# Down-projection of a dense SwiGLU layer: activation splits placed ahead of weight splits, and one chunk instead of two half-size chunks at the head of each half

## The chip, the cores and the metric

The kernel runs as one program on one core of a Trainium2 chip. The metric is the device time of one execution in microseconds (us), from launch to the last output. The core has a matrix engine (TensorE, PE in the profile; its weight loads are PEld), three elementwise engines (VectorE is DVE, ScalarE is ACT, GpSimd is POOL) and SyncE (SP), which here issues the transfers from device memory. Each engine takes its own instructions strictly in the order of the program and waits on counting semaphores that other engines raise.

## The reference, cut to what matters

Two layers of a diffusion backbone over 256 latent and 256 context tokens, all in float32. Layer 0 ends in a dense SwiGLU, layer 1 in a mixture of experts. The change touches only the last matrix product of the dense SwiGLU, that of `wd`:

```python
D_MODEL = 1024; SEQ = 256; CTX_LEN = 256; D_FF = 2816

def swiglu(h, wg, wu, wd):
    return (jax.nn.silu(h @ wg) * (h @ wu)) @ wd

# layer 0, for the latent tokens x and the context tokens ctx alike:
f_x = swiglu(ln_modulate(x, sh2x, sc2x), w_ff_gate[0], w_ff_up[0], w_ff_down[0])
x = ln_affine(ALPHA * x + gt2x * f_x, ln2_g[0], ln2_b[0])
```

## The kernel before, in words

A float32 product is made of three faster ones: each operand is split into a high part (a rounded copy) and a low part (operand minus high part), and `mm3` (L836) issues high x high, high x low and low x high. So every weight chunk must be split before TensorE can use it. ScalarE copies it to `w_hi` (`split_hi`, L1594), and then VectorE makes three quarters of `w_lo` and GpSimd the last quarter, at the same time (the two `split_lo`, L2020 and L2620). `w_lo` lies over `ring`, where the chunk landed. The ring has 4 slots of 2048 floats per partition (1 MB), `w_hi` has 3 buffers (HIS). The activations `a_t` of the down-projection are split too: `down_hi` on ScalarE (L1850) and `down_lo` on VectorE (L2312) write `a_hi` and `a_lo`, two buffers each.

The inner dimension 2816 is 22 tiles of 128 (FT). `DOWN` cuts it into six groups: one of 2 tiles at the head, then five of 4. The product is made in two halves, first the latent tokens (half 1), then the context tokens (half 0), with all weights read twice. So there are 12 groups, g = 0 to 11, and g = 6 is the head of the second half. A group has two chunks, dh = 0 and 1, one for each half of the 1024 output columns. A chunk of a full group is 4 tiles x 512 columns (1 MB) and takes 4 tiles x 2 token blocks x 3 = 24 matmuls; a chunk of a head group is 2 tiles x 512 columns (512 KB) and takes 12. q_down is the number, among all split chunks, of the first chunk of the down-projection.

What sets the order, engine by engine:
- TensorE waits at each group for `as_hi` and `as_lo` (the activations are split) and at each chunk for `lo_dve` and `lo_pool` (the weights are split). The last matmul of a chunk raises `w_used`; at the end of a half that matmul raises `fd_mm` instead, and `w_used` comes with the next matmul.
- ScalarE and VectorE run, for each group g: the splits of the two chunks of group g + 1, then the split of the activations of group g + 1, and in the second half a piece of the residual addition and layer norm of the latent tokens (`add_half`, `norm_a`, `norm_b`, `modulate`).
- `split_hi(q)` waits until chunk q - 3 is used, since it takes that chunk's `w_hi` buffer. The split of the second chunk of group g + 1 therefore waits for the first chunk of group g. `down_hi(g)` waits until group g - 2 is used.
- SyncE loads chunk n into the ring when chunk n - 4 is used. GpSimd runs its parts of the splits one after another.
- Ahead of the down-projection, the first two of its chunks are split inside the loop over gate and up projections. The second of these on VectorE stands between the last activation product (L2305) and `down_lo(0)`.
- In group 10 TensorE transposes the two normed latent tiles (`turn_tile`, the second one behind the second chunk); the second waits for `modulate` of the first tile on ScalarE and VectorE (`h_t`, L1624 and L2039). After the down-projection it goes on to the input projection of layer 1 for the latent tokens, with weights `in_w_in`.

Of the kernel before, what the change touches and what calls it, by code (L numbers as in the profile page):

```python
# [30 lines left out]
D = 1024  # L31
# [20 lines left out]
FT = D_FF // P  # L52
# [182 lines left out]
def ring_chunks(w):  # L235

    chunks = []

    def mod(l, cb):
        v = w["w_mod"][l].rearrange("(h k p) n -> h p k n", h=2, p=P)  # L240
        for h in range(2):
            chunks.append((("mod", l, cb, h), [(0, (4, 512), v[h, :, :, cb * 512:(cb + 1) * 512])]))

    def rows(name, v, k, c0, n):
        chunks.append((name, [(0, (k, n), v.rearrange("(k p) n -> p k n", p=P)[:, :, c0:c0 + n])]))

    for cb in EARLY_MOD:
        mod(0, cb)
    for l in range(DEPTH):
        w_in = w["w_in"][l]  # L250
        in_cols = ((0, Q_LORA), (OFF_KV, KV_LORA + ROPE), (OFF_F, 2 * FC), (OFF_F + 2 * FC, 2 * FC))
        for ch in IN_ORDER[l]:
            rows(("in", l, ch), w_in, KD, *in_cols[ch])
        if l == 0:
            for cb in FOURIER_MOD.values():
                mod(0, cb)
        for g in range(4):
            uq = w["w_uq"][l].rearrange("(k p) n -> p k n", p=P)[:, :, g * 4 * QK:(g + 1) * 4 * QK]
            uk = w["w_uk"][l][:, g * 4 * NOPE:(g + 1) * 4 * NOPE]
            uv = w["w_uv"][l][:, g * 4 * VH:(g + 1) * 4 * VH]  # L260
            chunks.append((("heads", l, g), [(0, (2, 4 * QK), uq), (2 * 4 * QK, (256,), uk),
                                             (2 * 4 * QK + 256, (256,), uv)]))
        for u, (kind, jj) in enumerate(MERGE):
            src, k, c0 = {"ga": (w_in, KD, OFF_G), "gf": (w_in, KD, OFF_G + D), "ao": (w["w_ao"][l], KD, 0),
                          "fo": (w["w_fo"][l], FG, 0)}[kind]
            rows((kind, l, jj), src, k, c0 + jj * 256, 256)
            if u in MERGE_MOD:
                mod(l, MERGE_MOD[u])
        v = w["w_out"][l].rearrange("(g k p) n -> g p k n", k=4, p=P)
        for dh in range(2):  # L270
            for kk in range(2):
                chunks.append((("out", l, dh, kk), [(0, (4, 512), v[kk, :, :, dh * 512:(dh + 1) * 512])]))
        if l == 0:
            for fp in range(FT // 2):
                rows(("fg", fp), w["w_ff_gate"][0], KD, fp * 256, 256)
                rows(("fu", fp), w["w_ff_up"][0], KD, fp * 256, 256)
                if 2 <= fp < 8:
                    mod(1, fp - 2)
            down = w["w_ff_down"][0].rearrange("(f p) n -> p f n", p=P)
            for half in (1, 0):  # L280
                for fg, n in DOWN:
                    for dh in range(2):
                        chunks.append((("fd", half, fg, dh), [(0, (n, 512), down[:, fg:fg + n, dh * 512:(dh + 1) * 512])]))
    return chunks

DOWN = [(0, FT % 4)] + [(f, 4) for f in range(FT % 4, FT, 4)]
assert FT % 4 and FT % 2 == 0  # L290


IN_ORDER = ((0, 1, 2, 3), (0, 2, 3, 1))
# [46 lines left out]
def build(nc, w, out):  # L340
    ctx = ExitStack()
    with ctx:
# [95 lines left out]
        a_hi = over("a_hi", [P, 2, 4, SEQ], at_a)  # L438
# [158 lines left out]
        w_used = sem("w_used")  # L597
# [224 lines left out]
        def _(pe):  # L822
# [373 lines left out]
            def dense_mixer():  # L1196
# [17 lines left out]
                for hx, half in enumerate((1, 0)):  # L1214
                    for i, (fg, n) in enumerate(DOWN):
                        g = len(DOWN) * hx + i
                        if g == 0:
                            pe.wait_ge(mod_done, mod_at[(1, 5)] + 1)
                        pe.wait_ge(as_hi, g + 1)
                        pe.wait_ge(as_lo, g + 1)  # L1220
                        for dh in range(2):
                            v = split_chunk(("fd", half, fg, dh), (n, 512))
                            order = [(f, t) for f in range(n) for t in range(2)]
                            if i == len(DOWN) - 1:
                                order = [(f, t) for t in range(2) for f in range(n)]
                            for f, t in order:
                                end = fg + f == FT - 1
                                cols = slice(t * P, (t + 1) * P)
                                mm3(psum[:, ff_bank(2 * half + t, dh), :],
                                    (a_hi[:, g % 2, f, cols], a_lo[:, g % 2, f, cols]), [x[:, f, :] for x in v],  # L1230
                                    start=(fg + f == 0), stop=end, sig=fd_mm if end else None,
                                    free=w_used if (f, t) == order[-1] else None)
                            if half == 0 and i == 4:
                                turn_tile(2, dh, 2 + dh)

# [335 lines left out]
        def _(act):  # L1571
# [129 lines left out]
            for l in range(DEPTH):  # L1701
# [133 lines left out]
                if l == 0:  # L1835
# [14 lines left out]
                    def down_hi(g):  # L1850

                        fg, n = DOWN[g % len(DOWN)]
                        c0 = SEQ if g < len(DOWN) else 0
                        if g >= 2:
                            act.wait_ge(w_used, q_down + 2 * (g - 1))
                        act.wait_ge(fa_done, fg + n)
                        act.activation(a_hi[:, g % 2, 0:n, :], a_t[:, fg:fg + n, c0:c0 + SEQ], ACT.Copy).then_inc(as_hi, 1)

                    act.wait_ge(fu_mm, FT)
                    down_hi(0)  # L1860
                    for g in range(2 * len(DOWN)):
                        for q in (q_down + 2 * g, q_down + 2 * g + 1):
                            if q + 2 < q_end:
                                split_hi(q + 2)
                        if g + 1 < 2 * len(DOWN):
                            down_hi(g + 1)
                        i = g - len(DOWN)
                        n = stats_before[2]
                        if i in (1, 2):
                            std(n + i - 1)  # L1870
                        elif i == 3:
                            std(n + 2)
                            std(n + 3)
                        elif i in (4, 5):
                            modulate(1, 1, i - 2, tiles_before[2] + i - 4)
# [103 lines left out]
        def _(dve):  # L1979
# [163 lines left out]
            for l in range(DEPTH):  # L2143
# [151 lines left out]
                if l == 0:  # L2295
# [21 lines left out]
                        low(a_lo[:, g % 2, 0:n, :], a_t[:, fg:fg + n, c0:c0 + SEQ], a_hi[:, g % 2, 0:n, :]).then_inc(as_lo, 1)  # L2317

                    down_lo(0)
                    for g in range(2 * len(DOWN)):  # L2320
                        for q in (q_down + 2 * g, q_down + 2 * g + 1):
                            if q + 2 < q_end:
                                split_lo(q + 2)
                        if g + 1 < 2 * len(DOWN):
                            down_lo(g + 1)
                        i = g - len(DOWN)
                        n = stats_before[2]
                        if i == 0:
# [447 lines left out]
```

## Time and profile before

| | |
|---|---|
| time, median of 3 runs | 2342.35 us (2335.09 to 2345.68) |
| the profiled execution: its time | 2342.66 us |
| its span, first to last instruction | 2340.8 us |
| mean granted TensorE clock | 0.946 |
| TensorE busy / VectorE busy / ScalarE busy / GpSimd busy | 90% / 41% / 32% / 26% |
| the down-projection | 840.06 to 986.10 us, 528 matmuls of 128x128 by 128x512 |

The profiled execution lies 0.3 us above the median of the runs, and its span is 1.9 us shorter than its time. Granted clock 1.00 means 2.4 GHz, and 0.5 means 1.2 GHz. Busy times of a matmul overlap the next one's: the distance from start to start is the true pace, 0.227 us for the 512 columns of this product at full clock.

### The profile page before, as it was taken

How to read it: one execution, taken by the hardware profiler on the slowest of the kernel's cores; microseconds unless marked ns; L12 is line 12 of the kernel's file. 1: busy time of each engine (PE TensorE's matmuls, PEld its weight loads, DVE VectorE, ACT ScalarE, POOL GpSimd, SP SyncE). 2: the span in 40 equal slices, each digit the busy share in tenths (PEclk: the TensorE clock that was granted, in tenths of full speed). 3: DMA queues.
4: the chain of work that ended last, by engine and by line, in shares of the span. 5: the costliest groups of instructions: out<-in, count | busy, mean ns of one | idle time of the engine just before them, and what ended most of it. 6: DMA issues, size and time to landing. Idle time of an engine off the chain costs nothing.

```text
span 2340.8 us, 33031 instructions
## 1 busy us (share of the span) xinstructions
PE 2095.2 (90%) x13045; PEld 1432.0 (61%) x13045; DVE 969.1 (41%) x1448; ACT 744.1 (32%) x1005; POOL 599.5 (26%) x344
## 2 busy tenths in 40 slices
PE   6988889993999988988788679999989999998886
PEld 3444467782877766755486555666565666666664
DVE  2244521256222334844423654333443323445445
ACT  2035532233121233324533222233232223333442
POOL 0012312150122234202323213333212333233431
PEclk8999999995999999999899779999999999999997
DMA  7311025440254334411067158999977999989994
GB/s 269 95 41 37 19 71 178 144 147 18 91 197 163 126 127 161 155 46 54 19 218 250 41 223 338 396 404 419 380 287 310 392 403 421 384 320 382 420 415 165
DMA packets 157247, 510.65 MB, mean 218 GB/s; under 512 B 8460, under 2 KB 72076, under 8 KB 113956
## 3 DMA queue, kind: packets, MB, share of 16 engines
q1 hardware_dynamic: 157092, 508.50, 57.1%
q8 instruction: 108, 1.77, 0.3%
q14 instruction: 47, 0.39, 0.0%
HBM read 507.42 MB, written 1.05 MB: 217 GB/s over the span
## 4 chain that ended last, share of the span: by engine, by line
PE 72%; DVE 9%; issue 8%; POOL 4%; DMA 4%; ACT 3%; SPq 0%; DVEq 0%; POOLq 0%; ACTq 0%
PE psum L829 69%; POOL w_lo L2675 2%; POOL reg_p L2650 1%; PE psum L1113 1%; DVE stat L2221 1%; DMA e_ring<-in_experts 1%; ACT w_hi L1600 1%; DVE w_lo L2018 1%; DVE reg_q L2214 1%; DMA ring<-in_w_ao 1%; DMA ring<-in_w_in 0%; DMA ring<-in_w_out 0%; DMA ring<-in_w_ff_down 0%; PE psum L1500 0%; PE psum L920 0%
## 5 line engine op out<-in xcount | busy, mean ns | idle before, releaser
L2675 POOL TENSOR_TENSOR w_lo<-e_ring,w_hi 128x512 fp32r<-128x512 f32 x92 | 215.1, 2340 | 540.4 <-PE psum L829 332.6
L2627 POOL TENSOR_TENSOR w_lo<-ring,w_hi 128x512 fp32r<-128x512 f32 (+1 forms) x86 | 200.7, 2335 | 592.2 <-ACT w_hi L1600 592.0
L829 PE MATMUL psum<-e_ring,reg_q 128*32 128x128 f32 (+3 forms) x4272 | 303.9, 333 | 12.3 <-DVE reg_q L2544 3.3
L2018 DVE TENSOR_TENSOR w_lo<-ring,w_hi 128x1536 fp32r<-128x1536 f32 (+1 forms) x86 | 149.5, 1742 | 380.4 <-ACT w_hi L1600 380.2
L1600 ACT ACTIVATE w_hi<-ring 128x2048 fp32r<-128x2048 f32 (+1 forms) x86 | 154.1, 1794 | 401.3 <-PE psum L829 104.3
L829 PEld LDWEIGHTS psum<-e_ring,reg_q 128*32 128x32 f32 (+1 forms) x4272 | 182.3, 120 | 118.5 <-issue 66.8
L2018 DVE TENSOR_TENSOR w_lo<-e_ring,w_hi 128x1536 fp32r<-128x1536 f32 x92 | 171.6, 1869 | 159.4 <-PE psum L829 138.1
L1922 ACT ACTIVATE w_hi<-e_ring 128x2048 fp32r<-128x2048 f32 x92 | 175.8, 1911 | 173.3 <-DMA e_ring<-in_experts 168.4
L829 PE MATMUL psum<-reg_q 96*128 96x512 f32 (+4 forms) x300 | 128.6, 558 | 18.7 <-ACT reg_v L1765 10.1
L829 PE MATMUL psum<-h_hi,w_hi 128*128 128x512 f32 x352 | 140.0, 398 | 5.5 <-issue 5.5
L829 PE MATMUL psum<-w_hi,xg_hi 128*128 128x512 f32 x336 | 138.9, 414 | 4.8 <-ACT w_hi L1922 3.2
L829 PE MATMUL psum<-e_more,reg_q 128*64 128x256 f32 (+3 forms) x1328 | 140.4, 401 | 0.0
L829 PE MATMUL psum<-h_lo,w_hi 128*128 128x512 f32 x352 | 137.8, 392 | 0.0
L829 PE MATMUL psum<-h_hi,w_lo 128*128 128x512 f32 x352 | 137.8, 391 | 0.0
L829 PE MATMUL psum<-w_hi,xg_lo 128*128 128x512 f32 x336 | 135.5, 403 | 0.0
L2675 POOL TENSOR_TENSOR w_lo_more<-e_more,w_hi 128x512 fp32r<-128x512 f32 x34 | 77.7, 2284 | 176.3 <-PE psum L829 154.4
L2650 POOL TENSOR_SCALAR reg_p<-reg_p,stat 128x512 f32<-128x512 f32 (+1 forms) x96 | 68.1, 709 | 198.8 <-DVE stat L2227 198.8
L1922 ACT ACTIVATE w_hi<-e_more 128x2048 fp32r<-128x2048 f32 x34 | 65.1, 1914 | 156.2 <-DMA e_more<-in_experts 142.9
L2221 DVE TENSOR_REDUCE stat<-psum 128x1 f32<-128x512 f32 (+1 forms) x96 | 57.7, 601 | 99.3 <-PE psum L829 98.1
L829 PE MATMUL psum<-g_hi,w_hi 128*128 128x512 f32 (+1 forms) x256 | 88.6, 346 | 9.4 <-issue 3.5
L829 PEld LDWEIGHTS psum<-e_more,reg_q 128*64 128x64 f32 (+1 forms) x1328 | 61.5, 122 | 56.9 <-issue 39.4
L829 PE MATMUL psum<-h_t,ring 128*128 128x512 f32 (+2 forms) x256 | 93.3, 525 | 3.0 <-ACT h_t L1658 2.4
(306 smaller groups left out, 3726.9 us busy)
## 6 DMA issues: line engine op xcount, KB each, us to landing
e_ring<-in_experts SPq DMA_DIRECT2D x240, 1024.0 KB, 9.4
e_more<-in_experts SPq DMA_DIRECT2D x96, 1024.0 KB, 9.4
ring<-in_w_mod SPq DMA_DIRECT2D x48, 1024.0 KB, 8.2
ring<-in_w_in SPq DMA_DIRECT2D x22, 1024.0 KB, 5.3
ring<-in_w_ff_down SPq DMA_DIRECT2D x20, 1024.0 KB, 5.0
ring<-in_w_ff_gate SPq DMA_DIRECT2D x11, 1024.0 KB, 5.3
ring<-in_w_ff_up SPq DMA_DIRECT2D x11, 1024.0 KB, 5.5
ring<-in_w_ao SPq DMA_DIRECT2D x8, 1024.0 KB, 5.6
```

The lines of the kernel that those rows point to most:

```text
L829: ins = pe.matmul(o, lhs, rhs, start=start, stop=stop, **kw)
L1113: ins = pe.transpose(psum[:, 4 + c % 2, k * P:(k + 1) * P], reg_p[:, c % 3, k * P:(k + 1) * P], ident)
L1600: act.activation(w_hi[:, q % HIS, 0:size], ring[:, n % SLOTS, 0:size], ACT.Copy).then_inc(hi_ok, 1)
L1922: act.activation(w_hi[:, (n_split + t) % HIS, :], e_slot[slot], ACT.Copy).then_inc(hi_ok, 1)
L2018: return dve.tensor_tensor(dst, src, hi.bitcast(F32), ALU.subtract)
L2214: ins = dve.tensor_tensor(q_t[64:96, g % 2, h, a:NTOK], rope_a[rows, a:NTOK], rope_b[rows, a:NTOK], ALU.add)
L2221: link(dve.reduce_max(s_top[:, c % 4:c % 4 + 1], psum[:, 2 + c % 2, 0:nk], AX.X))
L2627: pool.tensor_tensor(w_lo[:, n % SLOTS, a:size], ring[:, n % SLOTS, a:size], w_hi[:, q % HIS, a:size].bitcast(F32), ALU.subtract).then_inc ...
L2650: pool.tensor_scalar(reg_p[:, c % 3, 0:nk], reg_p[:, c % 3, 0:nk], s_inv[:, c % 4:c % 4 + 1], 1.0, ALU.mult, ALU.mult).then_inc(s_nrm, 1)
L2675: pool.tensor_tensor(lo_slot[slot][:, LO_DVE:SLOT], e_slot[slot][:, LO_DVE:SLOT], w_hi[:, (n_split + t) % HIS, LO_DVE:SLOT].bitcast(F32), ...
```

## The change

Three things change. (1) At the head of each half the two chunks of 2 tiles x 512 columns become one chunk of 2 tiles x 1024 columns (1 MB); TensorE's 24 matmuls of that group keep their order and take their columns from the one chunk. There are 22 chunks where there were 24. (2) ScalarE and VectorE now walk over chunks (`DOWN_GROUP`: group, is it the group's first chunk, is it the last): at the first chunk of group g they split the activations of group g + 1, and then the weight chunk two further on; at the second chunk of a full group they split only the weight chunk two further on; behind the last chunk comes the residual and norm work as before. (3) `down_hi` waits on `DOWN_DONE[g - 2]`, the number of chunks up to the end of group g - 2, which is the same point of TensorE's work as before.

```diff
@@ -278,16 +278,22 @@
                     mod(1, fp - 2)
             down = w["w_ff_down"][0].rearrange("(f p) n -> p f n", p=P)
             for half in (1, 0):
-                for fg, n in DOWN:
-                    for dh in range(2):
-                        chunks.append((("fd", half, fg, dh), [(0, (n, 512), down[:, fg:fg + n, dh * 512:(dh + 1) * 512])]))
+                for fg, n, cols in DOWN_CHUNKS:
+                    c0 = cols[0] * 512
+                    chunks.append((("fd", half, fg, cols[0]),
+                                   [(0, (n, 512 * len(cols)), down[:, fg:fg + n, c0:c0 + 512 * len(cols)])]))
     return chunks
 
 
 
 
 DOWN = [(0, FT % 4)] + [(f, 4) for f in range(FT % 4, FT, 4)]
-assert FT % 4 and FT % 2 == 0
+assert FT % 4 == 2
+DOWN_CHUNKS = [(0, 2, (0, 1))] + [(fg, 4, (dh,)) for fg, _ in DOWN[1:] for dh in range(2)]
+DOWN_GROUP = [(g, i == 0 or c[0] != DOWN_CHUNKS[i - 1][0], i + 1 == len(DOWN_CHUNKS) or DOWN_CHUNKS[i + 1][0] != c[0])
+              for h in range(2) for i, c in enumerate(DOWN_CHUNKS)
+              for g in (h * len(DOWN) + [f for f, _ in DOWN].index(c[0]),)]
+DOWN_DONE = [max(c for c, (k, _, _) in enumerate(DOWN_GROUP) if k == g) + 1 for g in range(2 * len(DOWN))]
 
 
 IN_ORDER = ((0, 1, 2, 3), (0, 2, 3, 1))
@@ -1219,7 +1225,9 @@
                         pe.wait_ge(as_hi, g + 1)
                         pe.wait_ge(as_lo, g + 1)
                         for dh in range(2):
-                            v = split_chunk(("fd", half, fg, dh), (n, 512))
+                            if i or dh == 0:
+                                v = split_chunk(("fd", half, fg, dh), (n, 512 if i else D))
+                            w0 = 0 if i else dh * 512
                             order = [(f, t) for f in range(n) for t in range(2)]
                             if i == len(DOWN) - 1:
                                 order = [(f, t) for t in range(2) for f in range(n)]
@@ -1227,9 +1235,9 @@
                                 end = fg + f == FT - 1
                                 cols = slice(t * P, (t + 1) * P)
                                 mm3(psum[:, ff_bank(2 * half + t, dh), :],
-                                    (a_hi[:, g % 2, f, cols], a_lo[:, g % 2, f, cols]), [x[:, f, :] for x in v],
+                                    (a_hi[:, g % 2, f, cols], a_lo[:, g % 2, f, cols]), [x[:, f, w0:w0 + 512] for x in v],
                                     start=(fg + f == 0), stop=end, sig=fd_mm if end else None,
-                                    free=w_used if (f, t) == order[-1] else None)
+                                    free=w_used if (f, t) == order[-1] and (i or dh) else None)
                             if half == 0 and i == 4:
                                 turn_tile(2, dh, 2 + dh)
 
@@ -1852,18 +1860,20 @@
                         fg, n = DOWN[g % len(DOWN)]
                         c0 = SEQ if g < len(DOWN) else 0
                         if g >= 2:
-                            act.wait_ge(w_used, q_down + 2 * (g - 1))
+                            act.wait_ge(w_used, q_down + DOWN_DONE[g - 2])
                         act.wait_ge(fa_done, fg + n)
                         act.activation(a_hi[:, g % 2, 0:n, :], a_t[:, fg:fg + n, c0:c0 + SEQ], ACT.Copy).then_inc(as_hi, 1)
 
                     act.wait_ge(fu_mm, FT)
                     down_hi(0)
-                    for g in range(2 * len(DOWN)):
-                        for q in (q_down + 2 * g, q_down + 2 * g + 1):
-                            if q + 2 < q_end:
-                                split_hi(q + 2)
-                        if g + 1 < 2 * len(DOWN):
+                    for c, (g, first, last) in enumerate(DOWN_GROUP):
+
+                        if first and g + 1 < 2 * len(DOWN):
                             down_hi(g + 1)
+                        if q_down + c + 2 < q_end:
+                            split_hi(q_down + c + 2)
+                        if not last:
+                            continue
                         i = g - len(DOWN)
                         n = stats_before[2]
                         if i in (1, 2):
@@ -2317,12 +2327,13 @@
                         low(a_lo[:, g % 2, 0:n, :], a_t[:, fg:fg + n, c0:c0 + SEQ], a_hi[:, g % 2, 0:n, :]).then_inc(as_lo, 1)
 
                     down_lo(0)
-                    for g in range(2 * len(DOWN)):
-                        for q in (q_down + 2 * g, q_down + 2 * g + 1):
-                            if q + 2 < q_end:
-                                split_lo(q + 2)
-                        if g + 1 < 2 * len(DOWN):
+                    for c, (g, first, last) in enumerate(DOWN_GROUP):
+                        if first and g + 1 < 2 * len(DOWN):
                             down_lo(g + 1)
+                        if q_down + c + 2 < q_end:
+                            split_lo(q_down + c + 2)
+                        if not last:
+                            continue
                         i = g - len(DOWN)
                         n = stats_before[2]
                         if i == 0:
```

ScalarE around the head of the first half, before. `a_hi` is `down_hi`, `w_hi` is `split_hi` (128x1024 is a half-size chunk), `reg_f` a sigmoid of the gate projection:

```order
264 L1600 ACTIVATE w_hi<-ring 128x1024
265 L1842 ACTIVATE reg_f<-psum 128x512 x2
266 L1600 ACTIVATE w_hi<-ring 128x1024
267 L1857 ACTIVATE a_hi<-reg_q 128x512
268 L1600 ACTIVATE w_hi<-ring 128x2048 x2
269 L1857 ACTIVATE a_hi<-reg_q 128x1024
270 L1600 ACTIVATE w_hi<-ring 128x2048 x2
271 L1857 ACTIVATE a_hi<-reg_q 128x1024
```

The same place of the changed kernel:

```order
263 L1608 ACTIVATE w_hi<-ring 128x2048 x2
264 L1850 ACTIVATE reg_f<-psum 128x512 x2
265 L1608 ACTIVATE w_hi<-ring 128x2048
266 L1865 ACTIVATE a_hi<-reg_q 128x512
267 L1865 ACTIVATE a_hi<-reg_q 128x1024
268 L1608 ACTIVATE w_hi<-ring 128x2048
269 L1865 ACTIVATE a_hi<-reg_q 128x1024
270 L1608 ACTIVATE w_hi<-ring 128x2048 x2
```

The activations of group 1 now follow those of group 0 at once. From group 2 on (the `a_hi` of the next to last row) the activations of a group stand ahead of both its weight chunks, where they stood behind both.

VectorE at the same place, before, beginning with the last activation product of the up projection (L2305); `a_lo` is `down_lo`, `w_lo` is `split_lo`:

```order
447 L2305 TENSOR_TENSOR reg_q<-reg_f,psum 128x512
448 L2018 TENSOR_TENSOR w_lo<-ring,w_hi 128x768
449 L2018 TENSOR_TENSOR a_lo<-reg_q,a_hi 128x512
450 L2018 TENSOR_TENSOR w_lo<-ring,w_hi 128x1536 x2
451 L2018 TENSOR_TENSOR a_lo<-reg_q,a_hi 128x1024
452 L2018 TENSOR_TENSOR w_lo<-ring,w_hi 128x1536 x2
```

And after:

```order
446 L2315 TENSOR_TENSOR reg_q<-reg_f,psum 128x512
447 L2028 TENSOR_TENSOR w_lo<-ring,w_hi 128x1536
448 L2028 TENSOR_TENSOR a_lo<-reg_q,a_hi 128x512
449 L2028 TENSOR_TENSOR a_lo<-reg_q,a_hi 128x1024
450 L2028 TENSOR_TENSOR w_lo<-ring,w_hi 128x1536
451 L2028 TENSOR_TENSOR a_lo<-reg_q,a_hi 128x1024
```

The weight split ahead of the first activation split has twice the columns, and the activations of group 1 are split directly behind those of group 0.

VectorE at the head of the second half, before; `reg_r` and `x_res` (L2074, L2075) are the residual addition of the first latent tile:

```order
462 L2018 TENSOR_TENSOR w_lo<-ring,w_hi 128x1536 x2
463 L2018 TENSOR_TENSOR a_lo<-reg_q,a_hi 128x1024
464 L2074 TENSOR_TENSOR reg_r<-psum,gate 128x512
465 L2075 SCALAR_TENSOR_TENSOR x_res<-x_res,reg_r 128x512
466 L2074 TENSOR_TENSOR reg_r<-psum,gate 128x512
467 L2075 SCALAR_TENSOR_TENSOR x_res<-x_res,reg_r 128x512
468 L2018 TENSOR_TENSOR w_lo<-ring,w_hi 128x1536 x2
469 L2018 TENSOR_TENSOR a_lo<-reg_q,a_hi 128x1024
```

After:

```order
461 L2028 TENSOR_TENSOR a_lo<-reg_q,a_hi 128x1024
462 L2028 TENSOR_TENSOR w_lo<-ring,w_hi 128x1536
463 L2084 TENSOR_TENSOR reg_r<-psum,gate 128x512
464 L2085 SCALAR_TENSOR_TENSOR x_res<-x_res,reg_r 128x512
465 L2084 TENSOR_TENSOR reg_r<-psum,gate 128x512
466 L2085 SCALAR_TENSOR_TENSOR x_res<-x_res,reg_r 128x512
467 L2028 TENSOR_TENSOR a_lo<-reg_q,a_hi 128x1024
468 L2028 TENSOR_TENSOR w_lo<-ring,w_hi 128x1536 x2
```

The activation split of group 7 (the first row of after) stands ahead of the weight split instead of behind two of them, and that of group 8 ahead of two weight splits. The residual work keeps its place behind the last weight split of its group.

## Rows read from the trace of the kernel before

**Rows 1.** The page, chain that ended last: share of the span by engine

```profile
PE 72%; DVE 9%; issue 8%; POOL 4%; DMA 4%; ACT 3%; SPq 0%; DVEq 0%; POOLq 0%; ACTq 0%
```

**Rows 2.** Windows, each half: length, busy (instructions) of each engine, PEclk, DMA share, GB/s

```profile
840.06:911.36 71.30, 64.35 (x264) 51.46 (x265) 31.77 (x18) 26.51 (x18) 31.59 (x12) 0.95 0.48 163
911.36:986.10 74.74, 64.35 (x280) 51.87 (x279) 54.98 (x57) 28.69 (x28) 24.21 (x10) 0.95 0.50 169
```

**Rows 3.** Timeline, TensorE, group 0 to group 1: start, duration, instruction, idle before, releaser

```profile
846.99 0.39 PE L829 MATMUL psum<-w_hi,a_lo 128*128 128x512 f32 x1
851.55 0.77 PE L829 MATMUL psum<-w_hi,a_hi 128*128 128x512 f32 x1 [4.17 <-issue]
...
854.94 0.39 PE L829 MATMUL psum<-w_hi,a_lo 128*128 128x512 f32 x1
```

**Rows 4.** Timeline, TensorE, group 1 to group 2

```profile
863.81 0.39 PE L829 MATMUL psum<-w_hi,a_lo 128*128 128x512 f32 x1
864.89 0.47 PE L829 MATMUL psum<-w_hi,a_hi 128*128 128x512 f32 x1 [0.69 <-issue]
```

**Rows 5.** Timeline, TensorE, second half, into groups 7 and 10

```profile
916.59 0.39 PE L829 MATMUL psum<-w_hi,a_lo 128*128 128x512 f32 x1
922.92 0.76 PE L829 MATMUL psum<-w_hi,a_hi 128*128 128x512 f32 x1 [5.94 <-DVE a_lo L2018]
...
926.44 0.39 PE L829 MATMUL psum<-w_hi,a_lo 128*128 128x512 f32 x1
...
960.55 0.47 PE L829 MATMUL psum<-w_hi,a_hi 128*128 128x512 f32 x1 [1.12 <-issue]
```

**Rows 6.** Timeline, VectorE, its splits

```profile
838.29 0.95 DVE L2018 TENSOR_TENSOR w_lo<-ring,w_hi 128x768 fp32r<-128x768 f32 x1
...
849.15 2.29 DVE L2018 TENSOR_TENSOR a_lo<-reg_q,a_hi 128x1024 fp32r<-128x1024 f32 x1
...
860.80 1.76 DVE L2018 TENSOR_TENSOR w_lo<-ring,w_hi 128x1536 fp32r<-128x1536 f32 x1 [7.31 <-ACT w_hi L1600]
862.48 2.31 DVE L2018 TENSOR_TENSOR a_lo<-reg_q,a_hi 128x1024 fp32r<-128x1024 f32 x1
...
956.47 2.84 DVE L2018 TENSOR_TENSOR w_lo<-ring,w_hi 128x1536 fp32r<-128x1536 f32 x1
959.24 1.21 DVE L2018 TENSOR_TENSOR a_lo<-reg_q,a_hi 128x1024 fp32r<-128x1024 f32 x1
```

**Rows 7.** Timeline, ScalarE, its splits

```profile
847.35 1.04 ACT L1857 ACTIVATE a_hi<-reg_q 128x1024 fp32r<-128x1024 f32 x1
...
858.85 1.92 ACT L1600 ACTIVATE w_hi<-ring 128x2048 fp32r<-128x2048 f32 x1 [7.16 <-PE psum L829]
860.68 1.04 ACT L1857 ACTIVATE a_hi<-reg_q 128x1024 fp32r<-128x1024 f32 x1
```

**Rows 8.** Timeline, GpSimd, two of its splits

```profile
860.85 2.86 POOL L2627 TENSOR_TENSOR w_lo<-ring,w_hi 128x512 fp32r<-128x512 f32 x1 [6.22 <-ACT w_hi L1600]
...
956.09 1.61 POOL L2627 TENSOR_TENSOR w_lo<-ring,w_hi 128x512 fp32r<-128x512 f32 x1 [1.15 <-ACT w_hi L1600]
```

**Rows 9.** Timeline, TensorE, into group 0

```profile
837.20 0.39 PE L829 MATMUL psum<-h_hi,w_lo 128*128 128x512 f32 x1
840.06 0.47 PE L829 MATMUL psum<-w_hi,a_hi 128*128 128x512 f32 x1 [2.48 <-issue]
```

**Rows 10.** Line L761, the ring's transfers from 838 to 970 us

```profile
DMA to landing us min/median/max: 3.2/5.0/5.6
```

**Rows 11.** Windows, group 9, columns as in rows 2

```profile
948.27:960.55 12.28, 11.16 (x48) 8.93 (x49) 12.10 (x12) 4.97 (x4) 3.27 (x2) 1.00 0.50 172
```

**Rows 12.** Timeline, TensorE, the second transposition in group 10

```profile
972.43 0.60 PE L920 MATMUL psum<-const,xn 128*128 128x128 f32 x4
974.97 0.66 PE L920 MATMUL psum<-const,xn 128*128 128x128 f32 x4 [1.94 <-DVE h_t L2039]
```

**Rows 13.** Windows, in the attention of layer 1, columns as in rows 2

```profile
1120.00:1180.00 60.00, 47.67 (x251) 31.63 (x250) 22.40 (x51) 27.20 (x49) 16.25 (x15) 0.83 0.11 36
```

## The prediction

> **What bounds the kernel now.** The chain that ended last puts 72% of the span on TensorE [rows 1], so the first question is how much of the changed stage TensorE spends not multiplying. The two windows of the stage answer it: 71.30 and 74.74 us, 146.04 in all, with TensorE busy for 64.35 in each [rows 2]. The bare work is less than that, since busy times overlap: two matmuls in a row start 0.227 us apart, so the 264 matmuls of a half need 59.9 us. The first window counts just these 264, the second has 16 transpositions more. So 26 us of the stage are idle or half-speed time. The timeline of TensorE says where, and the timelines of VectorE, ScalarE and GpSimd, read backwards from each late start, say why.
>
> Into group 1 the last matmul of group 0 starts at 846.99 and the next at 851.55 [rows 3]. That is 4.56 us where 0.227 would do: 4.33 lost. VectorE's `a_lo` for group 1 starts at 849.15 and takes 2.29 us, so it ends at 851.44, 0.11 us ahead [rows 6]. ScalarE's `a_hi` for it started only at 847.35 [rows 7], behind two weight splits of which the second stood waiting for its chunk. Then TensorE runs at half speed: the 8 matmuls from 851.55 to 854.94 take 3.39 us instead of 1.81, another 1.58.
>
> Into group 2 the starts are 863.81 and 864.89, 0.85 us lost [rows 4]. The same pattern stands at the four full boundaries of the first half (idle 0.69 or 0.70 each). The cause in rows: when the first chunk of group 1 is used, ScalarE splits a weight chunk from 858.85 on, then makes `a_hi` from 860.68 to 861.72 [rows 7]; VectorE is in its own weight split from 860.80 on and takes `a_lo` from 862.48 to 864.79 [rows 6]. TensorE starts 0.10 us later. The profile calls these waits "issue"; the end of `a_lo` shows what they are.
>
> In the second half TensorE loses 6.10 us into group 7 (916.59 to 922.92, minus 0.227), where the profile itself names `a_lo`, and 1.71 to the half speed behind it (8 matmuls from 922.92 to 926.44 take 3.52 us) [rows 5]. The boundaries into groups 8 and 9 are as in rows 4 (0.69 and 0.70 idle), 0.85 each; into group 10 the idle time is 1.12 instead of 0.69, so 1.28 [rows 5].
>
> **The change, part by part.** All of it lies in this stage. Its end is passed on whole: TensorE goes straight on with the input projection of layer 1, whose weights are loaded when ring slots come free, and the context tiles' norms hang on the last groups.
>
> Activations first, first half. In the new order `a_hi` for group g + 1 waits only until group g - 1 is used, which is the start of group g. Take that start as zero: `a_hi` runs from 0.25 to 1.3, `a_lo` needs 1.21 or 2.31 us [rows 6] and ends at 2.5 to 3.6. It is needed at 10.9 (48 matmuls of 0.227). So the boundary waits go: 4.33 + 1.58 + 4 x 0.85 = 9.3 us.
>
> What is late next is the weight split that now stands behind. At 1.3 `w_hi` of the chunk two further on starts, takes 1.92 [rows 7], and the slower of its two low parts takes 2.86 on GpSimd [rows 8]: ready at 6.1, needed at 10.9. The chunk after it waits, as now, for the first chunk of the group (5.4) and is ready at 10.5, needed at 16.3. So 4.8 us of cover are left on each. The transfer: it is issued when the chunk four back is used and lands 5.0 us later [rows 10]; its split can't start until the chunk three back is used, 5.4 us after that issue. A landing would have to take over 10 us to be seen.
>
> The head chunk of full size costs something at the start. VectorE's weight split between the last activation product and `a_lo` of group 0 starts at 838.29 and takes 0.95 us for 768 columns [rows 6]; now it is the first chunk of group 1 with 1536 columns, 1.76 us [rows 6]. Group 0 waits for the `a_lo` behind it, so it starts 0.81 us later than 840.06 [rows 9]. The bounds are 0 and 1.9 (2.84, the dearest such split [rows 6]); I take 0.81, since GpSimd has done its part of that chunk while TensorE still works on the up projection. The idle time ahead of group 0 grows from 2.48 to 3.3 us; a half-speed stretch already follows it. I leave that as it is; it could cost 1.6 more or go. On ScalarE and in the loop ahead, the longer splits of 0.9 us hide under TensorE's matmuls, which run without a gap. One transfer of 1 MB instead of two of 512 KB, two instructions fewer per engine and one ring slot more ahead are worth nothing by themselves: nobody waits for a chunk there once `a_lo` is early.
>
> Sum of the first half: 9.3 - 0.8 = 8.5 us.
>
> Second half. The same gives 6.10 + 1.71 + 2 x 0.85 + 1.28 = 10.8 us, if VectorE keeps up, for here it also carries residuals and norms. I walked its queue with the durations of the rows. Group 7 brings one `a_lo`, two weight splits of 1.76 and 5.9 us of norm and residual: 10.7; groups 8 and 9 the same with 5.6 and 5.7. That is just under 10.9. Because `a_lo` stands ahead of the norm work of its group, it may lag: by the walk VectorE begins group 8's list 4.5 us after TensorE begins group 8, that of group 9 after 5.1 and that of group 10 after 5.7, always ahead of the 10.9 at which `a_lo` is due. In group 10 the list is short (6.1 us) and it catches up, but only just: the second transposition, which waits for VectorE's `h_t`, stays late. Now the wait there is 1.94 us [rows 12]; I get 1.4 to 3.4 and leave it, with ±1.5.
>
> A rule bears on this walk. The rows show `a_lo` at 2.31 us where GpSimd is splitting (860.85 to 863.71 [rows 8]), and at 1.21 where it isn't [rows 6]; and GpSimd's split at 2.86 beside VectorE's and 1.61 without [rows 8]. The Trainium skill, page "SBUF — State Buffer", section "Who interferes with whom", says that a VectorE instruction with two SBUF inputs and a GpSimd one that reads SBUF exclude each other, and the later one blocks fully. By that rule `a_lo`, now ahead of the weight split, should mostly find GpSimd idle; the trace agrees in so far as the price of meeting is about 1.1 us for one of the two.
>
> Total: 8.5 + 10.8 = 19.3 us. From the profiled execution's 2342.66 that makes 2323.4; the median of the runs is 0.3 lower. I say 2323.
>
> **The rivals.**
>
> *VectorE becomes the bound of the second half.* For it: in group 9 VectorE was busy for 12.10 of 12.28 us [rows 11], more than the 10.9 that TensorE needs, so if splits and norms still meet GpSimd each time, its queue sets the pace of groups 7 to 10. The second half would then be 5.4 + 4 x 12.1 + 10.9 + 3.4 for the transpositions = 68.1 us instead of 74.74, a gain of 6.6 instead of 10.8, and the time 2327.5. Against it: 2.2 us of those 12.10 are the meetings, and the new order takes at least one away.
>
> *The gain isn't passed on.* The stage ends early and what follows waits: for `in_w_in`, or for the context tiles' norms on VectorE. For it: the transfers are tied to used chunks, only 4 ahead. Against it: they land in 5.0 us and are needed 16 later, and the norm chain starts from the same last matmuls as before. All gone would be 2342.
>
> *Slower: the clock in later stages.* All later work is shifted by some 20 us and one head chunk fewer; the attention of layer 1 already runs at a granted clock of 0.83 in one window of 60 us [rows 13], so about a third of it at 1.2 GHz, because TensorE often waits there. Should such stretches grow by more than 39 us, the 19.3 would be gone; at 60 us more, 30 us lost, the time would be 2353. Against it: nothing in those stages changes its waits.
>
> **How the numbers follow.** Forecast 0.70, VectorE as bound 0.16, not passed on 0.10, slower 0.04. About 0.5% (11.7 us) is what a measurement of this kernel can tell from no change, so faster means under 2330.6. The forecast and nearly all of the second case lie there: 0.84; same 0.12, slower 0.04. Range: the low end takes the half speed behind the head (1.6) and the wait at the transposition (1.9) as gone, 2320, and 3 us for the spread of runs, whose lowest of before lay 7 us under the median: 2316. The high end takes the second case with a start 1.1 us later still and the transposition 1.5 later, 2330, and 3 us for spread: 2333.
>
> **What would show it.** Right: in the changed profile the down-projection takes about 126 us instead of 146; `a_lo` of every full group ends more than 5 us ahead of its first matmul, 1.2 us long in the first half; no idle time of TensorE above 0.3 us at boundaries in the first half; group 0 starts about 3.3 us behind the last up matmul; one half-speed stretch instead of three. Wrong: waits for `w_lo` at a chunk in the middle of a group (the weight split is late), gaps into groups 9 to 11 (VectorE is the bound), or a stage shorter by 20 us with the span unchanged (not passed on).

## The result, and the profile after

The changed kernel takes 2319.48 us (median of 5 runs, 2318.27 to 2322.26), against 2342.35 (median of 5, 2335.09 to 2345.68). The ratio is 0.9906, with a 95% interval of 0.9887 to 0.9926: between 17 and 26 us less. Its profiled execution takes 2319.48 us, with a span of 2317.6 and a mean granted clock of 0.951, where before had 2342.66, 2340.8 and 0.946. The forecast was 2323, with a range of 2316 to 2333.

First the stage as a whole, answering to [rows 2]. The windows of the changed kernel, within 0.3 us of the first matmul of each half and the first of what follows (length, busy and instructions of TensorE, its weight loads, VectorE, ScalarE and GpSimd, PEclk, DMA share, GB/s):

```profile
841.10:902.72 61.62, 61.62 (x265) 50.86 (x266) 25.86 (x17) 25.41 (x16) 31.47 (x11) 0.97 0.57 188
902.72:966.38 63.66, 61.73 (x281) 50.90 (x280) 51.67 (x56) 26.87 (x27) 20.66 (x9) 1.00 0.55 182
```

71.30 and 74.74 us have become 61.62 and 63.66. TensorE is busy for the whole first half and all but 1.93 us of the second. VectorE's busy time falls from 86.75 to 77.53 us with almost the same work: part of what counted as busy was waiting for GpSimd, as e6 below shows.

The timeline of TensorE, into groups 0, 1 and 2, answering to [rows 9], [rows 3] and [rows 4]:

```profile
841.10 0.49 PE L835 MATMUL psum<-w_hi,a_hi 128*128 128x512 f32 x1 [3.28 <-issue]
...
848.02 0.39 PE L835 MATMUL psum<-w_hi,a_lo 128*128 128x512 f32 x1
848.25 0.39 PE L835 MATMUL psum<-w_hi,a_hi 128*128 128x512 f32 x1
...
858.90 0.39 PE L835 MATMUL psum<-w_hi,a_lo 128*128 128x512 f32 x1
859.13 0.39 PE L835 MATMUL psum<-w_hi,a_hi 128*128 128x512 f32 x1
```

Group 0 starts 3.28 us of idle time behind the last up matmul, where it was 2.48; half speed follows in both (matmuls 0.43 us apart), about 1.6 us lost. Into groups 1 and 2 the matmuls follow at 0.23 us without a break, and so at every boundary up to group 10. The timeline of VectorE beside it, answering to [rows 6]:

```profile
838.54 1.75 DVE L2028 TENSOR_TENSOR w_lo<-ring,w_hi 128x1536 fp32r<-128x1536 f32 x1
840.21 1.82 DVE L2028 TENSOR_TENSOR a_lo<-reg_q,a_hi 128x512 fp32r<-128x512 f32 x2
843.63 1.76 DVE L2028 TENSOR_TENSOR w_lo<-ring,w_hi 128x1536 fp32r<-128x1536 f32 x1 [1.60 <-ACT w_hi L1608]
849.54 1.23 DVE L2028 TENSOR_TENSOR a_lo<-reg_q,a_hi 128x1024 fp32r<-128x1024 f32 x1 [4.15 <-ACT a_hi L1865]
```

The weight split ahead of group 0's activations is the longer one (1.75 us). The next row is two activation splits in one, those of groups 0 and 1: the second is done at 842.03, 6.2 us before group 1 begins at 848.25. That of group 2 ends at 850.77, 8.4 us before 859.13. Each takes 1.2 us instead of 2.3.

VectorE in the second half. Each of its lists begins with the activation split of the next group, and TensorE begins groups 8, 9 and 10 at 918.97, 929.85 and 940.73:

```profile
904.17 1.23 DVE L2028 TENSOR_TENSOR a_lo<-reg_q,a_hi 128x1024 fp32r<-128x1024 f32 x1 [2.77 <-ACT a_hi L1865]
...
910.92 1.22 DVE L2028 TENSOR_TENSOR a_lo<-reg_q,a_hi 128x1024 fp32r<-128x1024 f32 x1
...
923.99 1.22 DVE L2028 TENSOR_TENSOR a_lo<-reg_q,a_hi 128x1024 fp32r<-128x1024 f32 x1
...
935.18 1.22 DVE L2028 TENSOR_TENSOR a_lo<-reg_q,a_hi 128x1024 fp32r<-128x1024 f32 x1
936.32 5.61 DVE L2028 TENSOR_TENSOR w_lo<-ring,w_hi 128x1536 fp32r<-128x1536 f32 x2
...
947.49 1.23 DVE L2028 TENSOR_TENSOR a_lo<-reg_q,a_hi 128x1024 fp32r<-128x1024 f32 x1
```

No activation split is late, but VectorE falls further behind from group to group.

The one wait left in the second half, answering to [rows 12]:

```profile
955.15 0.66 PE L926 MATMUL psum<-const,xn 128*128 128x128 f32 x4 [1.93 <-DVE h_t L2049]
```

By first matmuls, the first half is 9.8 us shorter but starts 0.8 us later behind the up projection; the second went from 75.0 (911.38 to 986.4) to 63.9 us (902.65 to 966.6), 11.1 less. That makes 20.0 us. From there to the expert stage the shift is passed on whole: the first expert product moves from 1373.1 to 1353.3. The span is 23.2 us shorter, and the other 3.5 lie in the expert stage, from the first to the last scatter product (the matmuls that put the experts' results back in token order): 942.3 us before, 938.8 after. e5 below is about these.

### The profile page after: what moved, and what is told of

Read it like the earlier page. It is cut to its first block, busy times and chain, and to the rows that moved or that the text cites. A ratio compares the mean times of both kernels' runs of the same rounds, so it can differ in the third digit from the quotient of the medians.

```text
span 2317.6 us, 33019 instructions
## 1 busy us (share of the span) xinstructions
PE 2081.4 (90%) x13045; PEld 1426.2 (62%) x13045; DVE 963.1 (42%) x1446; ACT 743.9 (32%) x1003; POOL 595.3 (26%) x342
## 4 chain that ended last, share of the span: by engine, by line
PE 73%; issue 8%; DVE 8%; POOL 5%; DMA 4%; ACT 2%; SPq 0%; DVEq 0%; POOLq 0%; ACTq 0%
PE psum L835 70%; POOL w_lo L2686 3%; POOL reg_p L2661 1%; PE psum L1119 1%; DMA ring<-in_w_mod 1%; DVE stat L2231 1%; DMA e_ring<-in_experts 1%; DVE reg_q L2224 1%; DMA ring<-in_w_ao 1%; ACT w_hi L1608 1%; DMA ring<-in_w_out 0%; DMA ring<-in_w_in 0%; DVE w_lo L2028 0%; PE psum L1508 0%; PE psum L926 0%
```

## The experiments

"Stage" is the distance between the starts of the first and last `w_hi,a_hi` matmul of the down-projection: 145.6 us before, 124.8 after. It leaves out the 0.8 us by which group 0 starts later in the kernels with the full-size head chunk. "Expert stage" is that between the first and last `y_hi,sel_slot` matmul. Ratios are to the kernel before on the same chip, with 95% intervals.

**e1: the order alone.** The kernel before, still with two half-size chunks at each head:

```diff
                     for g in range(2 * len(DOWN)):
+                        if g + 1 < 2 * len(DOWN):
+                            down_hi(g + 1)
                         for q in (q_down + 2 * g, q_down + 2 * g + 1):
                             if q + 2 < q_end:
                                 split_hi(q + 2)
-                        if g + 1 < 2 * len(DOWN):
-                            down_hi(g + 1)
```

and the same with `down_lo` and `split_lo` on VectorE.

> The kernel before with the activation splits ahead of the weight splits, head groups still in two half-size chunks. Theory (TensorE waited for a_lo, which stood behind two weight splits): the gain is all here, about 20 us, 2322 against 2342; group 0 starts at 840.1 as in before; a remaining wait of up to 1 us into group 7, whose first weight chunk is split late behind the half-size chunks. Rival (the waits at the heads were a lack of weights, which the full-size chunk cures by reaching further ahead in the ring): the waits of 4.3 and 6.1 us into groups 1 and 7 stay, only the six boundary waits of 0.85 to 1.3 go, gain 5.5 us, 2337.

Measured: 2323.0 us, ratio 0.9917 (0.9902 to 0.9933), stage 129.7. The waits into groups 1 and 7 are gone as such; of the second 1.15 us from start to start is left, for which the profile names GpSimd:

```profile
908.50 0.39 PE L829 MATMUL psum<-w_hi,a_lo 128*128 128x512 f32 x1
909.65 0.47 PE L829 MATMUL psum<-w_hi,a_hi 128*128 128x512 f32 x1 [0.77 <-POOL w_lo L2627]
```

So the cause that the theory names holds, and the rival falls. Its size does not quite: all of the gain, about 20 us, was expected here. The median is 18.6 us below that of before, but the stage only 15.9 us shorter; the rest is spread outside the stage. The stage is 4.9 us longer than that of the whole change. Boundaries account for 0.9 into group 7 and 0.8 into group 9 (931.31 to 932.38), and most of the rest is at the transpositions:

```profile
956.74 0.63 PE L920 MATMUL psum<-const,xn 128*128 128x128 f32 x4 [1.10 <-ACT h_t L1624]
959.29 1.11 PE L920 MATMUL psum<-const,xn 128*128 128x128 f32 x4 [1.92 <-DVE h_t L2039]
960.06 0.78 PE L829 MATMUL psum<-w_hi,a_hi 128*128 128x512 f32 x1
960.63 0.63 PE L829 MATMUL psum<-w_lo,a_hi 128*128 128x512 f32 x1
```

The second one waits first for ScalarE and then for VectorE, 1.2 us longer in all, and the matmuls behind it last 0.63 us and start 0.43 apart: half speed, up to 962.26, another 1.3. These make 4.3 of the 4.9 us.

**e2: the full-size head chunk alone.** The changed kernel with the order of before:

```diff
                     for c, (g, first, last) in enumerate(DOWN_GROUP):
-                        if first and g + 1 < 2 * len(DOWN):
-                            down_lo(g + 1)
                         if q_down + c + 2 < q_end:
                             split_lo(q_down + c + 2)
                         if not last:
                             continue
+                        if g + 1 < 2 * len(DOWN):
+                            down_lo(g + 1)
```

and the same with `down_hi` and `split_hi` on ScalarE.

> The changed kernel with the order of the splits as before (weights of the next group, then its activations), head groups in one chunk. Theory: one weight split fewer stands ahead of the activations of groups 1 and 7, so the wait into group 1 goes and that into group 7 shrinks from 6.1 to under 1 us with no half-speed stretch behind it; the boundary waits of 0.85 stay at all full groups; group 0 starts 0.8 us later; gain 11 to 13 us, 2330. Rival (only the weights' prefetch matters): gain as large as that of the whole change less the boundary waits, 14 us; rival (merging does nothing without the order): waits of 4.3 and 6.1 us stay, no gain, 2343.

Measured: 2333.55 us, ratio 0.9965 (0.9952 to 0.9978), stage 135.3. The timeline of TensorE, into groups 2 and 7:

```profile
860.83 0.47 PE L835 MATMUL psum<-w_hi,a_hi 128*128 128x512 f32 x1 [0.69 <-issue]
...
914.56 0.47 PE L835 MATMUL psum<-w_hi,a_hi 128*128 128x512 f32 x1 [0.92 <-issue]
```

The wait into group 1 is gone, that into group 7 is 1.08 us instead of 6.10, and the waits of 0.85 us stand at the full boundaries as before. Merging works by the same cause as the order: with one weight split per head group there is one fewer ahead of the next activations. The stage gained 10.3 us, 9.5 with the later start of group 0, where I expected 11 to 13, and the median 8. Two small terms were left out: a wait of 0.54 us into group 6 (907.18 to 907.95), and again a half-speed stretch behind the second transposition:

```profile
964.97 1.07 PE L926 MATMUL psum<-const,xn 128*128 128x128 f32 x4 [1.94 <-DVE h_t L2048]
965.69 0.77 PE L835 MATMUL psum<-w_hi,a_hi 128*128 128x512 f32 x1
966.26 0.63 PE L835 MATMUL psum<-w_lo,a_hi 128*128 128x512 f32 x1
```

From 965.69 to 968.67, 7 matmuls take 2.98 us instead of 1.59.

So the parts are not a sum. The order alone takes 15.9 us off the stage, the chunk alone 10.3, both together 20.8: they cut the same waits at the heads. What the chunk adds to the order is 4.9 us, the wait into group 7 and later ones in the second half; 0.8 of it goes again in the later start of group 0. These worths are read from one trace of each part: by the ratios, 0.9917 for the order alone against 0.9906 and, in e5, 0.9913 for the whole change, the times don't tell the two apart.

**e3: group 0 earlier.** The changed kernel with VectorE's split of the first full weight chunk behind the first activation split:

```diff
-                        split_lo(q_ffn + 2 * fp + 3)
+                        if fp < FT // 2 - 1:
+                            split_lo(q_ffn + 2 * fp + 3)
...
                     down_lo(0)
+                    split_lo(q_down + 1)
```

> The changed kernel, with VectorE's split of the first full weight chunk moved from ahead of the activation split of group 0 to behind it. Theory (group 0 starts late because that split of 1.75 us stands in front): group 0 starts 1.7 us earlier, 1.6 us behind the last up matmul instead of 3.3; the half-speed stretch behind it (1.6 us) goes or stays, so 1.7 to 3.3 us less than the changed kernel. Rival (ScalarE or the waits of TensorE's queue set that start): no earlier.

Measured: 2317.75 us, ratio 0.9901 (0.9886 to 0.9915), stage 123.2. TensorE's first matmul of group 0:

```profile
841.90 0.47 PE L835 MATMUL psum<-w_hi,a_hi 128*128 128x512 f32 x1 [1.61 <-ACT a_hi L1865]
```

The idle time ahead is 1.61 us instead of 3.28 and no half speed follows, which takes 1.6 us off the stage as well: 3.3 by the trace. By the ratios (0.9901 against 0.9906 and, in e5, 0.9913 for the changed kernel) the two are too near to be told apart by times alone.

**e4: e3, and the modulation ahead of the last weight split.** On ScalarE and VectorE:

```diff
+                        if last and g == 2 * len(DOWN) - 2:
+                            modulate(1, 1, 2, tiles_before[2])
                         if q_down + c + 2 < q_end:
                             split_lo(q_down + c + 2)
...
-                        elif i in (4, 5):
-                            modulate(1, 1, i - 2, tiles_before[2] + i - 4)
+                        elif i == 5:
+                            modulate(1, 1, 3, tiles_before[2] + 1)
```

> As e3, and in group 10 the modulation of the first latent tile on ScalarE and VectorE stands ahead of the split of the last weight chunk. Theory: TensorE's wait of 1.93 us at the second transposition goes, and the last weight chunk, split some 3 us later, is still ready 2 us before it is needed: 2 to 2.2 us less than e3, about 2316 by the profile's time of the changed kernel. Rival (VectorE's queue is full there and pays elsewhere): a wait for w_lo in the last group in place of the one removed, no gain over e3.

Measured: 2313.64 us, ratio 0.9888 (0.9874 to 0.9903), stage 120.9. It is the lowest median of all, though by the ratios its interval overlaps those of e3 and of the changed kernel. VectorE in group 10:

```profile
946.05 1.76 DVE L2030 TENSOR_TENSOR w_lo<-ring,w_hi 128x1536 fp32r<-128x1536 f32 x1 [0.58 <-ACT w_hi L1608]
947.73 1.36 DVE L2051 TENSOR_SCALAR h_t<-psum,modcol 128x128 f32<-128x128 f32 x4
949.24 1.76 DVE L2030 TENSOR_TENSOR w_lo<-ring,w_hi 128x1536 fp32r<-128x1536 f32 x1 [0.15 <-ACT w_hi L1608]
```

`h_t` is ready at 949.09, just before TensorE comes to the second transposition (949.26). The last weight chunk is ready on VectorE at 951.00 and on GpSimd at 952.14, and is first used in the second half of group 11, from 955.58 on. The rival falls; 2.3 us of the stage went.

**e5: the changed kernel again.** No edit.

> The changed kernel again, beside before on the same chip. The down-projection gave 20 us by the two profiles, the span 23.2. Theory (the other 3 us are the spread of the expert stage from run to run): the stage again takes 124.8 us from first to last matmul, and the expert stage lies anywhere from 938 to 942 us in this run as in those before; median ratio 0.990 to 0.993. Rival (the change also shortens the expert stage, by the two chunks fewer in the ring and w_hi): the expert stage is again 3 to 4 us shorter than in every profile of before's chunk lists.

Measured: 2320.41 us (2319.21 to 2330.83), ratio 0.9913 (0.9893 to 0.9932), stage 124.8, the same to a tenth. The expert stage took 936.3 us here. Over all profiles it took 942.3 (before), 938.8 and 936.3 (changed), 939.1 (e1), 942.3 (e2), 939.0 (e3), 938.3 (e4), 938.5 (e6) and 939.9 (e7). The 936.3 lies below the 938 that I had given as the low end. The kernels with the chunk list of before are at 942.3, 939.1 and 938.5, those with the new one from 936.3 to 942.3. So the 3.5 us are spread from run to run, and no effect of the two chunks fewer can be seen. The time up to the down-projection spreads as well: its first matmul came between 839.5 and 849.8 us.

**e6: GpSimd out of the weight splits.** The kernel before, VectorE making all but 8 columns of each chunk of the down-projection:

```diff
-                m = size * 3 // 4
+                m = size - 8 if chunks[n][0][0] == "fd" else size * 3 // 4
```

and the same bound on GpSimd.

> The kernel before, with VectorE making all but 8 columns of the low part of each down-projection chunk and GpSimd only those 8. Theory (a_lo took 2.3 us because GpSimd's split of 1.2 us ran inside it, and VectorE stood meanwhile): a_lo of a full group takes 1.2 us, the weight split of 2040 columns 2.2 to 2.3, so a_lo ends 0.5 us earlier than before and the boundary wait shrinks from 0.85 to about 0.3 us, though VectorE has a third more elements of the weights. Rival (a_lo is slow by itself at that place, by its operands): a_lo stays at 2.3 us, the boundary waits grow to 1.4 us.

Measured: 2334.06 us in one run, stage 139.0. VectorE at the end of group 1, and GpSimd beside it:

```profile
862.60 2.28 DVE L2018 TENSOR_TENSOR w_lo<-ring,w_hi 128x2040 fp32r<-128x2040 f32 x1 [6.45 <-ACT w_hi L1600]
864.80 1.22 DVE L2018 TENSOR_TENSOR a_lo<-reg_q,a_hi 128x1024 fp32r<-128x1024 f32 x1
```

```profile
862.64 2.30 POOL L2627 TENSOR_TENSOR w_lo<-ring,w_hi 128x8 fp32r<-128x8 f32 x1 [6.43 <-ACT w_hi L1600]
```

`a_lo` takes 1.22 us instead of 2.31 and the boundary wait is 0.29 us instead of 0.85, as the theory said. GpSimd needed 2.30 us for 8 columns: it stood through VectorE's whole instruction. What I had not looked for: the stage is 6.6 us shorter than in before. VectorE splits a chunk, all but 8 columns of it, in 2.28 us, while the two together took 2.91 (860.80 to 863.71 [rows 6, 8]), so in this place GpSimd's quarter bought nothing. With one run, the whole kernel's time says less than the stage. The Trainium skill, page "SBUF — State Buffer", section "Who interferes with whom", has this as an exclusive use of the shared read side by two-input instructions, the later one waiting; the trace agrees, with 2.30 beside 2.28 us.

**e7: more work for VectorE.** The changed kernel with the activation split of groups 7 to 11 done twice:

```diff
+                        if g > len(DOWN):
+                            link(low(a_lo[:, g % 2, 0:n, :], a_t[:, fg:fg + n, c0:c0 + SEQ], a_hi[:, g % 2, 0:n, :]))
                         low(a_lo[:, g % 2, 0:n, :], a_t[:, fg:fg + n, c0:c0 + SEQ], a_hi[:, g % 2, 0:n, :]).then_inc(as_lo, 1)
```

> The changed kernel with the activation split of groups 7 to 11 done twice on VectorE, 1.2 us more per group (up to 2.3 where it meets GpSimd). Theory (VectorE is near its limit in the second half, its lag behind TensorE grew to some 5 us of the 10.9 it has): no wait at the boundaries into groups 8 and 9; the lag is 5 us larger by group 10, so a wait of up to 1 us at the first transposition or the boundary into group 11, and the wait at the second transposition grows from 1.9 to 4 to 8 us. Rival (ample room on VectorE): nothing moves, the wait at the transposition stays within 1.3 us of 1.9.

Measured: 2331.88 us in one run, stage 134.0. TensorE into groups 9 and 10, and at the second transposition:

```profile
940.59 0.47 PE L835 MATMUL psum<-w_hi,a_hi 128*128 128x512 f32 x1 [1.89 <-DVE w_lo L2028]
...
954.00 0.47 PE L835 MATMUL psum<-w_hi,a_hi 128*128 128x512 f32 x1 [2.25 <-DVE w_lo L2028]
...
970.32 1.12 PE L926 MATMUL psum<-const,xn 128*128 128x128 f32 x4 [3.60 <-DVE h_t L2049]
```

The stage grew by 9.2 us for 1.2 to 2.3 us more in each of five groups. By start to start distances 2.0 and 2.4 us of it are the first two waits and 1.7 the longer wait at the transposition; most of the rest is half speed behind it (12 matmuls 0.43 us apart). The rival with ample room falls, but the theory was wrong on the place: I expected no wait into groups 8 and 9 and the bulk, 4 to 8 us, at the transposition, where 3.60 were measured. The wait is already there into group 9, and it is for `w_lo`, the weight split that now stands behind the activations, not for `a_lo`.

## Why the prediction was right, point by point

*Activations behind two weight splits.* Shown: e1 changes nothing but this order and takes 15.9 us off the stage. The forecast for the first half was 8.5 us and the profiles have 9.0; for the second 10.8, and 11.1. Both were a little low for the same reason: at a boundary of before I counted the wait alone, 0.85 us, but the matmuls right behind it start slower too (864.89, then 865.20, 0.31 us apart), and a whole group took 11.84 us (864.89 to 876.73) where it now takes 10.88, 0.96 less. The walk of the weight splits held in the first half: group 1 starts at 848.25, and the two chunks split beside it are ready on GpSimd at 854.25 and 858.80, 6.0 and 10.6 us later, where the walk had 6.1 and 10.5.

*`a_lo` shorter ahead of GpSimd's split.* Shown: 1.22 us in the changed kernel, and 1.22 in e6, where all but 8 columns of GpSimd's part were taken away. One reading was wrong, though. The prediction takes GpSimd's 1.61 us [rows 8] as a split without VectorE beside it. VectorE was splitting at the same time, from 956.47, and took 2.84 us instead of 1.76 [rows 6]: there VectorE was the one held. So either engine can be the one that pays, by 1.1 us.

*The late start of group 0.* The 0.81 us came as predicted (3.28 of idle instead of 2.48), and e3 shows the cause. I left the half-speed stretch behind it as it was, and it stayed. It too hung on that idle time: behind 2.48 and 3.28 us it was there, behind the 1.61 of e3 and e4 it was not.

*The head chunk worth nothing by itself.* This sentence of the prediction was wrong as worded. With early activations the chunk still adds 4.9 us (changed kernel against e1), part of it a half-speed stretch. I had not walked the order without the chunk: there the first weight chunk of group 7 is split late, and GpSimd is the last to be waited for. With the order of before it is worth 10.3 us, since it takes one weight split out of the way of `a_lo`.

*VectorE keeps up, only just.* The outcome was right, and the walk behind it was too kind. It said that VectorE's lists, from one activation split to the next, take just under the 10.9 us that TensorE needs; in the trace they take 13.1, 11.2 and 12.3 us (910.92 to 923.99, 935.18 and 947.49). It priced each weight split at 1.76 us, but of the last list both met GpSimd, 5.61 us for the two, as in group 9 of before: there the new order took no meeting away, which was the argument set against the first rival. Lists that short would not let VectorE fall further behind from group to group, and yet the walk had it 4.5, 5.1 and 5.7 us behind TensorE at groups 8, 9 and 10; the trace has 5.0 (923.99 against 918.97), 5.3 (935.18 against 929.85) and 6.8 (947.49 against 940.73). The rival had the pace nearly right (12.1 us per list; the three take 12.2 on average), but not what follows from it: it let TensorE run at that pace from group 7 on. In the trace VectorE begins the list of group 7 only 2.8 us behind TensorE (910.92 against 908.09), each list adds to that, and the half ends before the lag makes TensorE wait at a boundary. The transposition stayed late by 1.93 us, as left in the sum. e7 shows how near it was: with 1.2 to 2.3 us more per group, TensorE waits into groups 9 and 10.

*One sign failed.* The prediction said that every full group's `a_lo` ends more than 5 us ahead of its first matmul. In the first half it does (6.2 us for group 1, 8.4 for group 2), but not for groups 7, 9 and 10: there it ends 2.7 us (905.40 against 908.09), 4.6 and 4.3 us ahead. None was late, so the time did not show it.

*Passed on.* The first expert product came 19.8 us earlier. The rival of a later wait and that of a slower clock both fall: from the end of the down-projection to that product it is 386.72 us in both profiles, at a granted clock of 0.88 in both, and the window of the attention [rows 13], shifted, has 0.83 in both.

*The size.* 19.3 us were forecast, and the stage gave 20.0. The rest of the 22.9 between the medians is within the spread of the runs; in e5 the medians lie 21.1 apart. The low end of the range was added up a little too wide: its terms give 2316.6 to 2317, not 2316.

## What to carry to other kernels

When an engine runs several kinds of preparation for a consumer, put first what is ready to be made and due first. Here the activation split could start one group ahead, and it stood behind a weight split that had to wait for the consumer itself. A larger first chunk and a better order can cut the same waits: measure each alone before adding up their worth. Behind a reordering, ask which wait is next: here it was the weight split on VectorE (e7) and one transposition (e4). Moving one more weight split and one modulation gave a further 5.6 us by the traces. And before sharing a job between two engines, check that they can really do it at once: VectorE and GpSimd together took 2.91 us for a chunk that VectorE split nearly alone in 2.28 (e6).

## What the runs showed of the hardware that was not expected

Behind the same idle time of 1.92 to 1.94 us at the second transposition, the matmuls ran on at full speed in before, in the changed kernel twice, and in e3, but at half speed in e1 and e2 for some 2 and 3 us. The granted clock there depended on more than the length of the last wait. In e1 an idle time of 1.10 us lies shortly before, in e2 none, so the cause stays open. This half speed is part of what the stage lost in both, and no experiment here takes it away by itself.

VectorE's ten full-size activation splits of this stage count 22.0 us of busy time in before and 12.2 in the changed kernel and in e6. In the 9.8 us between them VectorE only stood for GpSimd. A duration of 2.3 us for 1024 columns, beside 1.2 elsewhere, was the sign of it.
